# Where the rounds of a top-k search stand: one tile's search in the projection, three rounds per level in the RWKV chunks

## The reference

```python
topk = min(IDX_TOPK_MAX, t // 4)          # 128
dots = jnp.einsum('bqhd,bsd->bqhs', qib, k_i).astype(jnp.float32) * IDX_DIM ** -0.5
score = jnp.einsum('bqhs,bqh->bqs', jax.nn.relu(dots), wib.astype(jnp.float32)) * IDX_HEADS ** -0.5
score = jnp.where(causal[None], score, -jnp.inf)
_, sel = lax.top_k(score, topk)
...
p = jax.nn.softmax(logits, axis=-1).astype(kv.dtype)
```

## Time and profile before

| what | value |
|---|---|
| median of 3 runs | 2016.34 us (2016.19 to 2020.74) |
| time of the profiled execution | 2005.66 us |
| its span, first to last instruction | 2003.9 us |
| mean granted TensorE clock | 0.907 of full speed |
| busy: PE, DVE, ACT, POOL | 1627.5, 664.0, 416.3, 153.0 us |

### The profile page before, as it was taken

One profiled execution on the slowest core, in us unless ns is written; L12 is line 12 of the kernel. 1 busy time (PEld: TensorE's weight loads), 2 busy tenths in 40 slices (PEclk: granted clock), 3 DMA queues, 4 the chain that ended last, 5 costly groups with the idle time before them and its releaser, 6 DMA issues. The chain is left out here.

```text
span 2003.9 us, 25681 instructions
## 1 busy us (share of the span) xinstructions
PE 1627.5 (81%) x10484; PEld 885.9 (44%) x10613; DVE 664.0 (33%) x1162; ACT 416.3 (21%) x742; POOL 153.0 (8%) x187
## 2 busy tenths in 40 slices
PE   7999567777969988788887599889789888788883
PEld 5666267654443333333332478654433333233331
DVE  4563866767231111111111633493411111111113
ACT  5333412225210100000001412472201000000001
POOL 0000401111010000000000100251100000000001
PEclk9999778987979999899899699999899889889996
DMA  5230600010858999999996521206679999999994
GB/s 160 74 82 1 126 2 3 2 51 36 335 207 339 399 398 402 401 405 404 403 401 270 210 84 43 84 1 237 267 281 402 404 406 390 396 389 393 394 390 153
DMA packets 101159, 492.30 MB, mean 246 GB/s; under 512 B 30896, under 2 KB 55472, under 8 KB 75952
## 3 DMA queue, kind: packets, MB, share of 16 engines
q1 hardware_dynamic: 88240, 461.26, 60.4%
q0 software_dynamic: 4608, 16.78, 2.1%
q10 hardware_dynamic: 8192, 12.59, 1.9%
HBM read 461.24 MB, written 29.36 MB: 245 GB/s over the span
## 5 line engine op out<-in xcount | busy, mean ns | idle before, releaser
L671 PE MATMUL ps<-w_unit,xT 128*48 128x512 f32 x1024 | 517.7, 665 | 137.5 <-DMA w_unit<-in_moe_w 134.9
L672 PE MATMUL ps<-w_unit,xT 128*48 128x512 f32 x1024 | 518.7, 666 | 0.0
L671 PEld LDWEIGHTS ps<-w_unit,xT 128*48 128x48 f32 x1024 | 135.0, 136 | 488.5 <-issue 485.4
L710 DVE TENSOR_TENSOR xT<-ps,gain 128x384 f32<-128x384 f32 x64 | 35.7, 557 | 731.9 <-PE ps L661 731.9
L700 PE MATMUL ps<-w_unit,hidT 128*48 128x512 f32 x512 | 235.8, 604 | 4.2 <-ACT hidT L727 3.2
L701 PE MATMUL ps<-w_unit,hidT 128*48 128x512 f32 x512 | 236.0, 604 | 0.0
L727 ACT ACTIVATE hidT<-ps 128x192 f32<-128x192 f32 x64 | 21.2, 331 | 640.1 <-PE ps L692 637.5
L1122 PE MATMUL ps<-hT_high,w_high 128*128 128x512 f32 (+1 forms) x344 | 140.3, 408 | 5.7 <-PE ps L1124 4.0
L1124 PE MATMUL ps<-hT_high,w_low 128*128 128x512 f32 (+1 forms) x344 | 136.7, 397 | 0.0
L1123 PE MATMUL ps<-hT_low,w_high 128*128 128x512 f32 (+1 forms) x344 | 136.5, 397 | 0.0
L672 PEld LDWEIGHTS ps<-w_unit,xT 128*48 128x48 f32 x1024 | 135.0, 136 | 0.0
(11 more groups left out here) (358 smaller groups left out, 2080.6 us busy)
## 6 DMA issues: line engine op xcount, KB each, us to landing
w_unit<-in_moe_w SPq DMA_DIRECT2D x188, 2048.0 KB, 37.9
x_rows<-sorted_rows SPq DMA_DIRECT2D x64, 192.0 KB, 41.5
expert_rows<-y ACTq DMA_DIRECT2D x128, 96.0 KB, 7.8
w_raw<-in_od_w_qkv SPq DMA_DIRECT2D x12, 1024.0 KB, 5.1
w_raw<-in_ev_w_in SPq DMA_DIRECT2D x10, 1024.0 KB, 5.4
w_unit<-in_moe_w SPq DMA_DIRECT2D x8, 1024.0 KB, 35.9
sorted_rows<-zero_rows SPq DMA_DIRECT2D x1, 6144.0 KB, 41.8
w_unit<-in_ev_w_out SPq DMA_DIRECT2D x2, 2048.0 KB, 10.5
```

Source lines behind the costliest of these rows:

```text
L671: nc.tensor.matmul(ps_1[b][0:MB, :], xT[b][:, k, :], w1[:, k, :], start=k == 0, stop=k == KD - 1)
L672: last = nc.tensor.matmul(ps_3[b][UP:UP + MB, :], xT[b][:, k, :], w3[:, k, :], start=k == 0, stop=k == KD - 1)
```

## The change

The sixteen rounds of tile 3 and their closing TENSOR_SCALAR move to the end of VectorE's work in `even_project`, behind a wait for the causal mask of that tile. The search in `rwkv_chunks` starts with tile 2. `PER_LEVEL` goes from (4, 4, 5, 6) to (3, 3, 3, 3) and `AT_LEVEL_4` from (1, 1, 2, 2) to (0, 1, 1, 1). With level 3 left out in the tiles 1 to 3, the chunks' levels held 13, 9, 12 and 14 rounds before, and hold 9, 7, 7 and 7 now. That leaves two rounds for `search.rest`.

```diff
@@ even_project
-    added, scored, own_pool = c.sem("added"), c.sem("scored"), c.sem("pool_own")
+    added, scored, own_pool, causal = c.sem("added"), c.sem("scored"), c.sem("pool_own"), c.sem("causal")
+    search = TopK(nc, c, ctx, m)
...
                 G_.affine_select(out=part, in_=part, compare_op=ALU.is_ge, fill=NEG, base=0,
-                                 pattern=[[-1, P]], channel_multiplier=1)
+                                 pattern=[[-1, P]], channel_multiplier=1).then_inc(causal, 1)
...
                 if ends_group(j) and g + 2 < NG:
                     split(g + 2)
-
-
+            dve.wait_ge(causal, 1)
+            search.rounds(dve, search.ROUNDS)
@@ TopK
-PER_LEVEL, AT_LEVEL_4 = (4, 4, 5, 6), (1, 1, 2, 2)
+PER_LEVEL, AT_LEVEL_4 = (3, 3, 3, 3), (0, 1, 1, 1)
...
-    def __init__(self, nc, c, ctx, m):
-        self.nc, self.m, self.r = nc, m, 0
+    def __init__(self, nc, c, ctx, m, tiles_done=0):
+        self.nc, self.m, self.r = nc, m, tiles_done * self.ROUNDS
@@ rwkv_chunks
-    search = TopK(nc, c, ctx, m)
+    search = TopK(nc, c, ctx, m, tiles_done=1)
```

## The result

The changed kernel takes 1994.28 us (median of 5 runs, 1990.91 to 2002.3), the kernel before 2016.19 us (median of 5, 2010.7 to 2020.74). The ratio is 0.9899, with a 95% interval of 0.9870 to 0.9927. Two later measurements gave 0.9916 (0.9883 to 0.9950) and 0.9900 (0.9858 to 0.9942). The change makes the kernel some 17 to 20 us faster. Medians are given only where no disturbed run is among them; ratios leave such runs out.

The account below looks back on a forecast made before the run. VectorE in program order was taken to bound the chunks' levels. -27.4 + 2.3 + 4.1 + 2.0 - 4.0 = -23.0 us takes 2016.3 us to 1993.3 us; forecast 1988 to 1999 us (0.65), wider range 1985 to 2003 us.

Parts of the forecast that it names:

- out of the levels: Chunks' levels: fewer search rounds on VectorE save 8.5, 3.4, 8.0 and 7.5 us in tiles 0 to 3, -27.4 us.
- end of the chunks: Last barrier of the chunks: two rounds and a close, 2.7 us, make VectorE end after ScalarE, +2.3 us.
- projection's barrier: End of the projection: of 24.8 us of search, 20.7 us hide behind matmuls and 4.1 us delay the barrier, +4.1 us.
- cold start of the preparation: Start of the preparation: TensorE, after standing 6.1 us, runs its first 4 us at 1.2 GHz, +2.0 us (0 to 3).
- clock in the tails: Tails between the levels: shorter TensorE stands bring back half the time lost to 1.2 GHz, -4 us; a loss possible.
- late product: Chunks' levels: a TensorE product late once in each of two tiles takes back 1 us at worst; nothing taken off.
- tile 1's close: Instruction closing tile 1's search: taken at 0.7 us, with 0.46 us, the one measured close, as the other end.
- 10.7 us between profile and median: Whole kernel: the runs' median lies 10.7 us above the profiled execution; the same difference was put on the forecast.
- all of the clock comes back: Rival, tails: busier levels keep every tail off 1.2 GHz; -27.3 us, or -29 us without the cold start; chance 0.13.
- the clock gives less: Rival, tails: they fall to the low clock in other places; -18 to -11 us, 1998 to 2005 us; chance 0.17.
- TensorE as the bound at 1.2 GHz: Rival, levels: TensorE at the low clock outlasts VectorE, kernel 23 us slower, 2039 us; chance 0.03.
- the search isn't hidden: Rival, projection: rounds start only after the `gate` matmuls, all 24.8 us before the barrier; 0 us, 2016 us; chance 0.02.

Follow-up runs that it names:

- dummy search: The kernel before plus 34 MAX8 over tile 3's 512 keys, results unread, at the end of VectorE's projection; ratio to the kernel before 1.0074 (1.0041 to 1.0107).
- e2: The changed kernel plus 80 small matmuls after TensorE's last projection product, while VectorE ends the search; ratio to the kernel before 0.9889 (0.9852 to 0.9927).
- e3: The changed kernel with 13 rounds in the projection, the other three and the close in tile 0's levels; ratio to the kernel before 0.9898 (0.9848 to 0.9948).
- f2: The changed kernel without the search in the projection, so tile 3 is not searched; ratio to the kernel before 0.9841 (0.9787 to 0.9895).
- f4: The changed kernel with 13 rounds for tile 3 in the projection and no search in the chunks; ratio to the kernel before 0.9796 (0.9748 to 0.9844).

## Why the prediction was right, and where it was not

The forecast was 1993.3 us and 23.0 us less; the runs gave 1994.28 us and 21.9 us less in the medians. For the profiled execution the forecast was 1982.7 us, and it took 1994.28 us, 11.6 us more. In the trace, up to the attention's start, the terms came out as follows.

| term | forecast, us | measured, us |
|---|---|---|
| out of the levels | -27.4 | -26.2 |
| end of the chunks | +2.3 | +2.2 |
| projection's barrier | +4.1 | +4.2 |
| cold start of the preparation | +2.0 (0 to 3) | +6.8 |
| clock in the tails | -4 (-8 to +6.6) | -3.7 |
| sum | -23.0 | -16.7 |

**What bounds.** VectorE in program order was the path through the levels, and each round there was paid in full. The tiles' levels came out at 15.0, 16.6, 14.8 and 14.8 us for forecasts of 14.7, 16.6, 14.4 and 14.4. The 0.36 us in the tiles 2 and 3 is the add of level 2 waiting for TensorE. That is the late product that I priced at 1 us in all and took nothing off for. The reason that I gave for 0.7 us for tile 1's close, fewer keys than in the close of 0.46 us, does not carry it; the value fits the levels before and is 0.4 us too much at the end. And TensorE still waits 2.33, 1.35, 1.82 and 1.16 us for the add in four of its seven waits in the levels, where I forecast mostly under 1 us.

**The cover in the projection.** 20.7 us hidden and 4.1 us not: right, and shown from the other side by the dummy search.

**The clock behind it is the term that was mis-sized.** The step failed where it said "if the first 4 us run at 1.2 GHz, 2 us are lost; nothing is the lower bound and 3 us the upper one". The cold stretch beside it had full matmuls. Here more than 10 us ran cold, through matmuls of 64 rows. By the time to the norm a cold start costs the changed kernel 5.7 to 7.0 us in three traces. By the time to the first add it is 6.8 us in the first trace against the first of before. Against e2, e3, f2 and f4, which took 75.1 to 75.4 us, it is 4.2 us in that trace, which was spared the second fall of the clock, and 5.6 to 7.1 us in the other two. The prediction gave "the preparation grows by more than 3 us" as a sign that its sum is wrong, and that sign came. All six traces with a stand of 6.3 us began the preparation at 0.50. Of the seven with a stand of 1.8 us, six stayed at 1.00, and one, the kernel before itself, did not. So the kernel before pays the cold start too in some executions, and the change makes it regular.

**Why the total was right all the same.** The trace of before on which the sum was made was a lucky one. At 2005.66 us it was shorter than every other run of that kernel (2007.0 us is the next). Its preparation was warm, and its part behind the chunks, 1562.0 us, was the shortest of fourteen executions (1562.0 to 1578.6 us). The second trace, at 2023.84 us, lies above the median instead. Against it the attention starts 25.1 us earlier, against the first 16.7 us. The mean of the two traces of before less the mean of the three of the changed kernel is 446.1 - 427.5 = 18.6 us, within the 17 to 20 us of the ratios. I had put the 10.7 us between profile and median on the forecast without knowing what they were. Part of them is shown now: 9.8 us of that spread sits in the expert layers and the second layer, and the cold preparation is another 5 to 7 us. The traces say where: over the expert layers TensorE waits 134.9 to 137.6 us for the weights' DMA (`in_moe_w`) in the seven executions with a rest of 1562.0 to 1567.4 us, and 142.9 to 148.5 us in the seven with 1568.7 to 1578.6 us. What makes that wait longer was not tried. The close agreement of 23.0 and 21.9 us is partly luck; the ratios say 17 to 20 us.

**The clock in the tails.** The sum of -4 us was met, and the part that repeats is tile 0's. With 12 or 13 rounds in its levels its tail took 25.2 to 26.3 us in five traces (median 26.0), and with 9 rounds 21.9 to 24.3 us in eight (median 22.9). Some 3 us are the change's. The other two tails go either way: tile 1's took 21.94 and 24.35 us in the two traces of before and 23.5 us in three of the changed kernel, tile 2's 23.98 and 23.37 us before and 21.94, 24.49 and 24.48 us after. That shorter stands bring the clock back by themselves is not shown: with no rounds at all (f4) each tail took 24.4 us.

**The rivals.** That all of the clock comes back fell. That the clock gives less, for -18 to -11 us, is nearest in number to the first trace's -16.7 us, but for another cause: it put the loss in the tails, which gave what I forecast, and the loss was in the preparation. TensorE as the bound at 1.2 GHz fell too, as the granted clock in the levels was 0.97 to 1.00. That the search isn't hidden fell with the barrier at 199.11 us.

## What to carry to other kernels

Work that is moved under another engine's cover should end before that engine does. The last three rounds, 5 us of VectorE, moved the barrier by only 4 us, but made TensorE stand and cost it the clock in the next stage, another 5.7 to 7.0 us up to the norm. To put them into tile 0's levels (e3) gave nothing that the runs could tell; they were free only in a wait. Look in the timeline for waits of the engine that carries the work, and cut the work to their sizes: 13 rounds in one, 3 in another and one at a time in short ones were worth 12.5 us more than 16 in one place and 2 at an end. How much of it each place gave was not tried. And before a sum is made against one trace, compare a second one of the same kernel.

## What the runs showed of the hardware

The granted clock stayed at 0.50 for over 10 us although TensorE was busy all the time, while it ran f32 matmuls of 64 x 128 (7.19 us for eight that take 3.70 us at 1.00). With 80 bf16 matmuls of 128 x 128 in front, it was back within 4 us; f32 matmuls of 128 rows and 8 columns (`squares`) brought it back too, in six traces. Whether the rows alone make the difference was not tried. The clock also fell to 0.50 after a stand of only 1.84 us, in one of seven executions, right as the 64-row matmuls began. And it fell with TensorE busy all the time, during f32 matmuls of 8 x 128 or just after them, in eleven of fourteen traces. The Trainium skill, page "TensorE: Matmul & The Clock Gate", section "HAM oscillation — how this bites in real kernels", lays the low clock to long idle gaps. The six executions with a stand of 6.3 us agree; the second trace of the kernel before, at 0.50 after 1.84 us, does not, nor does the first at 220 us, at 0.50 with no gap at all.
